# An encoder layer in float32 halves: the beginning, both starts of the gate-and-up products and the start of the down product are put in another order

## What is computed

```python
u = rms_norm(x, norm_mix_g)
proj = u @ w_in                                  # q, k, v, and three parts of the convolution
att = rms_norm(diff_attention(q, k, v, lam, rel_bias), subln_g) * (1 - lam_init)
conv = bg * short_conv(cg * hv, conv_w)
x = x + concat(att, conv) @ w_out
z = rms_norm(x, norm_ffn_g)
hid = silu(z @ w_gate) * (z @ w_up)
x = x + hid @ w_down
return rms_norm(x, final_g)
```

## Time and profile before

| | before |
|---|---|
| median of three runs | 2777.56 us |
| the profiled execution | 2776.66 us |
| its span | 2774.6 us |
| PE busy | 2664.3 us (96%) |
| DVE busy | 1511.8 us (54%) |
| ACT busy | 1020.9 us (37%) |
| mean granted clock of PE | 0.989 |

### The profile page before, as it was taken

How to read it: one execution, slowest core, us unless ns; L and a number is a source line. 1 busy time by engine, 2 the same in 40 slices (tenths; PEclk the granted TensorE clock), 3 DMA queues, 4 the chain that set the end, 5 groups by cost and what they waited for, 6 DMA issues and landing times. The chain is left out here.

```text
span 2774.6 us, 34571 instructions
## 1 busy us (share of the span) xinstructions
PE 2664.3 (96%) x12280; PEld 2182.5 (79%) x12280; DVE 1511.8 (54%) x2203; ACT 1020.9 (37%) x1429; POOL 500.7 (18%) x343
## 2 busy tenths in 40 slices
PE   7999999989999999999989999989999999999997
PEld 5788888867777777778868888878888878888886
DVE  4321122268788887844466666676666643434343
ACT  4210000047667776742333333343333323323232
POOL 1000000047777777720000000000000000000000
PEclk9999999999999999999989999999999999999999
DMA  5543111223031311047762222252222235556563
GB/s 166 150 121 95 57 38 38 61 61 75 24 78 43 76 49 31 24 167 217 226 216 80 83 87 76 83 174 91 74 84 91 72 125 148 169 177 206 147 203 115
DMA packets 260687, 298.29 MB, mean 108 GB/s; under 512 B 15200, under 2 KB 179552, under 8 KB 260608
## 3 DMA queue, kind: packets, MB, share of 16 engines
q1 hardware_dynamic: 255952, 287.24, 34.9%
q0 software_dynamic: 2304, 8.39, 0.7%
q10 hardware_dynamic: 2352, 1.64, 0.2%
HBM read 212.28 MB, written 84.93 MB: 107 GB/s over the span
## 5 line engine op out<-in xcount | busy, mean ns | idle before, releaser
L1780 PE MATMUL banks<-z_hi,w_hi 128*128 128x512 f32 x1204 | 470.1, 390 | 8.4 <-ACT p L966 5.5
L1780 PE MATMUL banks<-z_lo,w_hi 128*128 128x512 f32 x1204 | 469.4, 390 | 0.0
L1780 PE MATMUL banks<-z_hi,w_lo 128*128 128x512 f32 x1204 | 469.3, 390 | 0.0
L1576 PE MATMUL projected<-u_t_hi,w_part_hi 128*128 128x512 f32 (+1 forms) x768 | 301.1, 392 | 3.2 <-DVE conv_y L1117 1.7
L1576 PE MATMUL projected<-u_t_lo,w_part_hi 128*128 128x512 f32 (+1 forms) x768 | 300.1, 391 | 0.0
L1576 PE MATMUL projected<-u_t_hi,w_part_lo 128*128 128x512 f32 (+1 forms) x768 | 299.8, 390 | 0.0
L702 POOL TENSOR_TENSOR exp<-exp,exp 128x2048 f32<-128x2048 f32 x64 | 295.4, 4616 | 5.3
L1780 PEld LDWEIGHTS banks<-z_hi,w_hi 128*128 128x128 f32 x1204 | 226.8, 188 | 57.0 <-issue 5.9
L860 ACT ACTIVATE exp<-exp,neg_max 128x2048 f32<-128x2048 f32 x128 | 257.1, 2009 | 36.3 <-DVE neg_max L1259 35.3
L1780 PEld LDWEIGHTS banks<-z_lo,w_hi 128*128 128x128 f32 x1204 | 226.8, 188 | 47.1
L1780 PEld LDWEIGHTS banks<-z_hi,w_lo 128*128 128x128 f32 x1204 | 226.6, 188 | 47.1
(11 more groups left out here) (146 smaller groups left out, 4414.7 us busy)
## 6 DMA issues: line engine op xcount, KB each, us to landing
...
z_stage<-z_blocks SPq DMA_DIRECT2D x11, 1024.0 KB, 6.2
```

The lines of the kernel that those rows point to most:

```text
L1576: last = nc.tensor.matmul(projected[:, bank * BANK:(bank + 1) * BANK], w_part[w][:, r if w else HI_SLOT[r], kt], u_t[u][:, kt, rows], star ...
L1780: last = nc.tensor.matmul(c_bank[BANK_OF[k]], w_slot[k][w][:, kt], z_slot[k][z][:, kt], start=(kt == 0 and t == 0 and k in (0, 1, 3, 4)), ...
```

## The change

- **Beginning.** `keep_bias(2)` and `keep_bias(3)` stand on ACT behind the squares of the second block and the first copy out of PSUM instead of ahead of them. The making of lambda moves behind the blocks on DVE and ACT.
- **End of the row blocks, step 0.** On DVE `sum_z` of the last two pairs, on ACT `evacuate_z` of the last two row blocks, and on SP `store_z` of the last two pairs move to steps 1 and 2 (their pieces belong to the second half). The products use the PSUM banks 0 to 3 alone, so that 4 to 7 can hold the turned rows on. Block 3 is split ahead of the last row block's norm. Weight slots 5 and 6 and the silu tiles lie elsewhere. The SP loads of blocks 4 to 6 now follow the block 3 load with one row store between.
- **Second half.** Block 0 has a place of its own (z_next) and is split between steps 19 and 20. Block 1 comes through the stage, the others are fetched straight to their slots, each as soon as its product in step 21 is done. DVE splits block 1 behind k = 2 of step 21, 2 and 3 behind k = 5 and 6, and 4, 5 and 6 behind k = 0, 1 and 2 of step 22.
- **Down.** The first down chunk is split by DVE ahead of the last `combine`, by ACT the second ahead of the last silu, and SP loads chunks 2 and 3 ahead of the rows of the result (y_rows).

```diff
@@ -279 +279 @@
-        w_at = ((147456, 149504), (204288, 206336), (208384, 194048), (167936, 169984), (172032, 174080), (40960, 43008), (45056, 47104))
+        w_at = ((147456, 149504), (204288, 206336), (208384, 194048), (167936, 169984), (172032, 174080), (196096, 198144), (200192, 202240))
@@ -281 +281,3 @@
-        z_stage = [at(offset, f"z_stage_{i}", [P, 4, BANK]) for i, offset in enumerate((131072, 196096, 73728))]
+        z_stage = at(131072, "z_stage", [P, 4, BANK])
+        z_next = [at(65536 + 8192 * n, f"z_next_{'hi' if n == 0 else 'lo'}", [P, 4, BANK], F32R) for n in range(2)]
@@ -286,3 +288,3 @@
-        up_0 = at(65536, "up_0", [P, BANK])
-        silu_0 = at(67584, "silu_0", [P, BANK])
-        hid_stage = at(69632, "hid_stage", [P, 2, BANK])
+        up_0 = at(40960, "up_0", [P, BANK])
+        silu_0 = at(43008, "silu_0", [P, BANK])
+        hid_stage = at(45056, "hid_stage", [P, 2, BANK])
@@ -293,2 +295,2 @@
-        down_raw = at(73728, "down_raw", [P, 2, D])
-        hid_raw = at(196096, "hid_raw", [P, 2, BANK])
+        down_raw = at(131072, "down_raw", [P, 2, D])
+        hid_raw = at(12288, "hid_raw", [P, 2, BANK])
@@ -313 +315 @@
-        c_bank = [banks[:, b] for b in (0, 1, 4, 5)]
+        c_bank = [banks[:, b] for b in range(4)]
@@ -315 +317 @@
-        y_banks = [banks[:, b:b + 2].rearrange("p b n -> p (b n)") for b in (2, 6, 0, 4)]
+        y_banks = [banks[:, b:b + 2].rearrange("p b n -> p (b n)") for b in (4, 6, 0, 2)]
@@ -570 +572 @@
-                if n % 2 == 0 and n >= 2:
+                if n % 2 == 0 and 2 <= n < N_ROWS - 2:
@@ -596,4 +597,12 @@
-                sp.wait_ge(z_lo_ready, 7 + k - 2)
-                sp.wait_ge(z_stored[1], 16 * 28)
-                sp.wait_ge(rows_stored[k % 2], 16 * (N_ROWS // 2))
-                sp.dma_start(z_stage[k % 3][:, :, :], z_dram[1, k].rearrange("k p t -> p k t")).then_inc(z_loaded[k % 3], 16)
+                if k == 0:
+                    sp.wait_ge(z_stored[1], 16 * 28)
+                    place = z_next[1]
+                elif k == 1:
+                    sp.wait_ge(z_lo_ready, 4)
+                    place = z_stage
+                else:
+                    sp.wait_ge(product_ready, 7 * (F_CHUNKS - 1) + k + 1)
+                    place = z_slot[k][1]
+                dst = place[:, :, :] if k == 1 else place[:, :, :].bitcast(FP32)
+                sp.dma_start(dst, z_dram[1, k].rearrange("k p t -> p k t")).then_inc(z_loaded if k == 1 else z_placed[k], 16)
@@ -611,0 +621,6 @@
+            sp.wait_ge(w_lo_ready_2, 7)
+            load_gate_up(2, 0)
+            store_z(N_ROWS // 2 - 2)
+            gate_up_step(0, 0, 0, 0)
+            gate_up_step(0, 1, 1, 1, 3)
+            gate_up_step(0, 2, 2, 0, 4)
@@ -613,2 +628 @@
-            gate_up_step(0, 0, 0, 0, 2)
-            with sp.Fori(0, F_CHUNKS // 2 - 2) as pair:
+            with sp.Fori(1, F_CHUNKS // 2 - 2) as pair:
@@ -616,0 +631,2 @@
+            load_z_next(0)
+            load_z_next(1)
@@ -618,2 +633,0 @@
-            for k in range(3):
-                load_z_next(k)
@@ -623 +637 @@
-            for k in range(3, 6):
+            for k in range(2, 5):
@@ -625,0 +640 @@
+            load_z_next(5)
@@ -654,0 +670 @@
+            load_down(0, 2, 0)
@@ -655,0 +672 @@
+            load_down(0, 3, 1)
@@ -659 +676 @@
-            with sp.Fori(1, F_CHUNKS // 2) as pair:
+            with sp.Fori(2, F_CHUNKS // 2) as pair:
@@ -798,4 +814,0 @@
-            keep_bias(2)
-            keep_bias(3)
-            act.wait_ge(lam_summed, 2)
-            nc.scalar.activation(lam_exp[:, :], lam_sum[:, :], ACT.Exp).then_inc(lam_exped, 1)
@@ -808,0 +822,3 @@
+                if first:
+                    keep_bias(2)
+                    keep_bias(3)
@@ -819,0 +836,2 @@
+            act.wait_ge(lam_summed, 2)
+            nc.scalar.activation(lam_exp[:, :], lam_sum[:, :], ACT.Exp).then_inc(lam_exped, 1)
@@ -949,3 +966,4 @@
-            def split_placed_z(k):
-                act.wait_ge(z_placed[k - 4], 16)
-                nc.scalar.activation(z_slot[k][0][:, :, :], z_slot[k][1][:, :, :].bitcast(FP32), ACT.Copy).then_inc(z_hi_ready, 1)
+            def split_placed_z(half, k):
+                hi, lo = z_next if half and k == 0 else z_slot[k]
+                act.wait_ge(z_placed[k], 32 if half and k >= 4 else 16)
+                nc.scalar.activation(hi[:, :, :], lo[:, :, :].bitcast(FP32), ACT.Copy).then_inc(z_hi_ready, 1)
@@ -998,0 +1017,4 @@
+                if n == N_ROWS - 1:
+                    act.wait_ge(o_summed, N_ROWS)
+                    split_z(0, 3)
@@ -1011,3 +1031,0 @@
-            act.wait_ge(o_summed, N_ROWS)
-            split_z(0, 3, 0, 4)
-            split_w(0, 0, 3, True)
@@ -1015,2 +1033,4 @@
-            split_w(0, 0, 4, True)
-            evacuate_z(N_ROWS - 1)
+            for k in range(3, 7):
+                split_w(0, 0, k, True)
+            for k in range(4, 7):
+                split_placed_z(0, k)
@@ -1020,9 +1039,0 @@
-            for k in range(5, 7):
-                split_w(0, 0, k, True)
-            split_placed_z(4)
-            split_placed_z(5)
-            split_w(1, 1, 0)
-            split_w(1, 1, 1)
-            split_placed_z(6)
-            act.wait_ge(z_stored[1], 16 * 28)
@@ -1030 +1041 @@
-            for k in range(2, 7):
+            for k in range(7):
@@ -1033 +1044,5 @@
-            with act.Fori(0, F_CHUNKS // 2 - 1) as pair:
+            gate_up_step(1, 1)
+            evacuate_z(N_ROWS - 2)
+            evacuate_z(N_ROWS - 1)
+            gate_up_step(2, 0)
+            with act.Fori(1, F_CHUNKS // 2 - 2) as pair:
@@ -1036,2 +1051,17 @@
-            gate_up_step(F_CHUNKS - 1, 1, lambda k: split_z(1, k, k % 3, (5, 1, 1)[k % 3] + k // 3))
-            with act.Fori(F_CHUNKS // 2, F_CHUNKS - 1) as pair:
+            gate_up_step(F_CHUNKS - 3, 1)
+            split_placed_z(1, 0)
+            gate_up_step(F_CHUNKS - 2, 0)
+            def next_z(step, k):
+                block = {(F_CHUNKS - 1, 1): 1, (F_CHUNKS - 1, 4): 2, (F_CHUNKS - 1, 5): 3, (F_CHUNKS - 1, 6): 4,
+                         (F_CHUNKS, 0): 5, (F_CHUNKS, 1): 6}.get((step, k))
+                if block == 1:
+                    split_z(1, 1)
+                elif block:
+                    split_placed_z(1, block)
+            gate_up_step(F_CHUNKS - 1, 1, lambda k: next_z(F_CHUNKS - 1, k))
+            gate_up_step(F_CHUNKS, 0, lambda k: next_z(F_CHUNKS, k))
+            gate_up_step(F_CHUNKS + 1, 1)
+            with act.Fori(F_CHUNKS // 2 + 1, F_CHUNKS - 1) as pair:
@@ -1060,2 +1089,0 @@
-            silu_second(STEPS - 1)
-            act.wait_ge(product_ready, 7 * STEPS)
@@ -1062,0 +1091 @@
+            silu_second(STEPS - 1)
@@ -1156,0 +1186,5 @@
+            norm_block(1, pieces=(0, 1))
+            dve.wait_ge(bias_stored, 16 * HEADS)
+            with dve.Fori(2, SB) as sb:
+                norm_block(sb, pieces=(0, 1, 2))
@@ -1164,9 +1197,0 @@
-            dve.wait_ge(lam_exped, 1)
-            nc.vector.tensor_tensor(lam_sum[:, 0:1], lam_exp[:, 1:2], lam_exp[:, 0:1], ALU.subtract).then_inc(lam_step, 1)
-            dve.wait_ge(lam_step, 1)
-            nc.vector.tensor_scalar(neg_lambda[:, :], lam_sum[:, 0:1], -LAM_INIT, None, ALU.add).then_inc(lam_step, 1)
-            norm_block(1, pieces=(0, 1))
@@ -1176,0 +1202,4 @@
+            dve.wait_ge(lam_exped, 1)
+            nc.vector.tensor_tensor(lam_sum[:, 0:1], lam_exp[:, 1:2], lam_exp[:, 0:1], ALU.subtract).then_inc(lam_step, 1)
+            dve.wait_ge(lam_step, 1)
+            nc.vector.tensor_scalar(neg_lambda[:, :], lam_sum[:, 0:1], -LAM_INIT, None, ALU.add).then_inc(lam_step, 1)
...
+            def split_z(half, k):
...
+                hi, lo = z_next if half and k == 0 else z_slot[k]
+                raw = z_stage[:, :, :] if (k == 1 if half else k < 4) else lo[:, :, :].bitcast(FP32)
+                dve.wait_ge(z_hi_ready, 7 * half + k + 1)
+                nc.vector.tensor_tensor(lo[:, :, :], raw, hi[:, :, :].bitcast(FP32), ALU.subtract).then_inc(z_lo_ready, 1)
@@ -1475,4 +1501,4 @@
-            for k in range(4, 7):
-                split_w(0, 0, k)
-            split_placed_z(4)
-            sum_z(N_ROWS // 2 - 1)
+            split_w(0, 0, 3)
+            split_w(0, 0, 4)
+            split_z(0, 4)
+            split_w(0, 0, 5)
@@ -1480 +1506,4 @@
-            split_placed_z(5)
+            split_w(0, 0, 6)
+            split_z(0, 5)
+            make_c_22(0)
+            split_z(0, 6)
@@ -1483 +1511,0 @@
-            make_c_22(0)
@@ -1489 +1516,2 @@
-            dve.wait_ge(z_stored[1], 16 * 28)
+            dve.wait_ge(rows_stored[0], 16 * (N_ROWS // 2))
+            dve.wait_ge(rows_stored[1], 16 * (N_ROWS // 2))
@@ -1499 +1527,5 @@
-            with dve.Fori(0, F_CHUNKS // 2 - 1) as pair:
+            sum_z(N_ROWS // 2 - 2)
+            gate_up_step(1, 1)
+            gate_up_step(2, 0)
+            sum_z(N_ROWS // 2 - 1)
+            with dve.Fori(1, F_CHUNKS // 2 - 2) as pair:
```

(62 more changed lines are left out.)

21 lines of the change are left out of this document (7 added, 14 removed).

## The result

The changed kernel takes 2752.74 us (median of 6, 2751.39 to 2755.57), the one before 2777.68 (6, 2774.94 to 2779.69): ratio 0.9913, interval 0.9902 to 0.9924. It is faster by 24.9 us, where 33 were forecast; the time lies 8.2 us above the forecast, at the end of the range: 2752.74 against 2753, while by the ratio it is a hair outside (0.9913, where 2753/2777.56 is 0.9912). The profiled execution took 2753.01 us, its span 2751.1 us, 23.5 less than before.

A forecast was written before the change was run, and what follows sets the result against it. PE bounds the kernel, losing time in stalls at four places and in the half clock behind them. Savings of 6.5 + 15.9 + 4.4 + 6.1 = 32.9 us off 2776.66 gave 2743.8, as median 2744.5, range 2738 to 2753 (8 in 10).

The forecast's parts named there:

- Beginning: Start to third block: PE's 5.48 us wait for u_tile and the half clock go; 6.5 us less.
- Step 0: Last row-block turn to step 2: blocks come earlier, only short PE waits remain, clock stays; 15.9 us less.
- rival of transfers that land together: Step 0: blocks 4 to 6 share the queues and come late, product 4 waits; 2750 us; chance 0.11.
- Step 21 to 22: Seam of the halves: one 4.6 us wait for u_3 with 2.8 us of half clock stays; 4.4 us less.
- Down: Start of down: first chunk ready 3.3 us earlier, half clock (2.6) and chunk 2's 0.2 us go; 6.1 us less.
- The y_rows are late next, but needed only at the group's end: Down: the result's row loads come later at no cost, within the term of 6.1 us less.
- the one on chunk 2's load: Down: chunk 2's load, issued at 2273.7 and no longer behind y_rows, saves the 0.2 us wait ahead of chunk 2.
- The sum: Whole kernel: the four places together take 32.9 us off the profiled execution's 2776.66, giving 2743.8; median forecast 2744.5.
- DVE stays the bound: Steps 0 to 2 and 21 to 22: waits for DVE return later, half of both seams' gain goes; 2757; chance 0.06.
- Short waits lower the clock: Step 0: 4 waits within 30 us cost one or two times 2.8 us of half clock; 2749; chance 0.09.
- Step 22 is better: Step 22: the clock stays or DVE is quicker than counted; 2740 us; chance 0.09.
- the slower rival: All loop steps: new banks and silu places slow each step, with 0.9 us a step 2783; chance 0.03.

The follow-up runs named there:

- e5: The kernel before with only the beginning part of the change (bias copies behind the squares, lambda behind the blocks): 2768.89 us, ratio 0.9972.
- second trace: The kernel before, unchanged, run and profiled once more: 2777.2 us (one run), span 2775.4.
- e8: The changed kernel with out_gain's wait at first use and, in step 22, DVE's u_3, block 6 and c_22 ahead of the next weight sums: 2738.86 us, 0.9866.

## Why the prediction was right or wrong

- **Beginning: right.** Forecast 6.5; the table gives 8.4 against the first trace and 7.4 against the second, e5 7.9 of median. 1.7 of the 8.4 lie ahead of the last four bias matmuls, and so ahead of the change's place; the second trace of the kernel before differs from the first by 1.5 there. From there on it is 6.7.
- **Step 0: right.** Forecast 15.9; last turn to step 2: 17.52 less 1.03, 16.5. Its inner waits were 0.23 and 0.91 where 0.7, 1.3 and 0.1 were forecast. The blocks came one behind the other, nearly when forecast: ACT had the last at 1408.61, and the forecast's 1414.5, less the 5.4 us by which this part is earlier, is 1409.1. The rival of transfers that land together is out. Step 1 then took 20.37 us, 1.3 more than a step without waits, where 0.9 was forecast.
- **Step 21 to 22: right, a size off.** Forecast 4.4; measured 3.5 + 2.2 = 5.7 (4.4 + 0.4 = 4.8 against the second trace). The wait was 4.18 (4.6), and the half clock behind it lasted 3.40 us and cost 1.7 (2.8).
- **Down: wrong, and this is the step that failed.** Forecast 6.1 less; measured 3.3 less and 6.9 more, 3.6 more. The first two halves held: the first wait is 0.59 us (0.7), and no half clock follows the start. The sentence that failed is "The y_rows are late next, but needed only at the group's end", with the one on chunk 2's load ahead of them: I followed chunk 2's data to DVE and not the instruction that stands ahead of its split, the wait for out_gain, whose load lies behind the same y_rows, and now behind chunk 3's too. The term is off by 9.7 us, the miss by 8.2. With the wait at its use the term is 3.32 + 2.90 = 6.2.
- **Attention: not the change.** The stretch is 3.1 us longer than in the first trace, but within 0.7 us of three others of the code before. A sum that is made against one execution carries this much error.
- **The sum.** By the spans 9.4 us are missing (23.5 for 32.9): 9.7 from down and 3.1 from the attention, while the beginning, step 0 and step 21 to 22 gave 3.8 more than forecast; 0.4 is small change. So the total came as near as it did partly by luck. The recorded 2744.5 is also 0.2 below its own sum (2743.8 + 0.9), and the 2757 of "DVE stays the bound" doesn't follow from its words: half of 15.9 + 4.4 is 10.2, so 2754.7.
- **The rivals.** "Short waits lower the clock": in step 0 it did not, 1.00 over the windows of steps 0 and 1; by the Trainium skill's rule ("TensorE: Matmul & The Clock Gate", "A second HAM failure mode") that was possible, and for these short waits the trace doesn't show it. "Step 22 is better" came only with e8, by another order. "DVE stays the bound" is out as it was put: step 1 gave back 1.0 us. The time that came out, near "transfers" and "DVE stays the bound", came by a mechanism that was none of them. That each loop step takes 19.04 us refutes the slower rival.
